# Attention scores of a hybrid decoder layer: three 64-row matmuls per block replaced by two 128-row matmuls with stacked query parts

## The chip, the cores and the metric

The kernel runs on one core of a Trainium2 chip. The metric is the device time of one execution in microseconds (us), as the median over several executions. Lower is better.

## The reference

The reference is one inference step of one decoder layer for a prompt of 512 positions and 8 sample positions of 2048 features: normalise, project to q, k, v and to the convolution's channels, dilated windowed attention over 16 heads of 64, a short gated convolution, an output projection, a gated feed-forward layer, and a per-layer embedding. What matters here is the score of the prompt's attention and the rows that are given back:

```
q = rms_norm(q.reshape(hs), q_norm)            # 16 heads of 64
k = rms_norm(k.reshape(hs), k_norm)
s = einsum('brnqhd,brnkhd->brnhqk', q, k) * HEAD_DIM ** -0.5 + bias
e = exp(s - max(s));  o = einsum('brnhqk,brnkhd->brnqhd', e, v) / sum(e)
outputs: y_prompt, y_sample, k_prompt (the keys), v_prompt (the values), ...
```

All is float32, and the kernel keeps that precision on TensorE by splitting each operand into a high part in fp32r (`hi`) and the rest (`lo`), and adding the products hi x hi, hi x lo and lo x hi.

## The kernel before

The work is laid out with features on the 128 partitions and the 520 positions along the free axis. Five engines run one program each and meet at semaphores: SP loads weights, ScalarE (ACT) writes the high part of each weight unit into `whi`, VectorE (DVE) writes the low part into `wlo`, TensorE (PE) multiplies, and GpSimd (POOL) keeps sums of squares and issues the stores and the smaller loads.

The first stage, "mixers", has eight head pairs j = 0 to 7. A pair has 12 weight units g = 0 to 11 (v, k, q and three convolution projections, two units each) of 48 matmuls of 260 columns. `whi` and `wlo` have four buffers, and ACT and DVE split unit g + 4 at step g. While pair j is projected, the attention of pair a = j - 1 is worked through, one slice after each unit (`attention(a, g)`); the last pair's attention lies in the convolution half of the output projection that follows. At g = 0 to 7 a score block is made: head e = g // 4 of the pair, query block qb = g % 4, against (qb + 1) x 128 keys, so 128, 256, 384 and 512 columns, twice. `products` issues hi x hi (L539), the weights `qhi` against `klo` (L540), and `qlo` against `khi` (L541). Their operands take 64 of the 128 partitions, those of the head. The same three lines, with 128 partitions, multiply values by probabilities (`vhi`, `vlo`, `pthi`, `ptlo`).

At g = 9, 10 and 11 of pair j (`heads`) the keys and queries of that pair are normalised, on DVE a reciprocal and a multiplication for each (L1405, L1407); ACT copies the high part of k (L936) and q (L918), DVE subtracts for the low part (L1374, L1330). PE transposes v and then k into one PSUM bank, ACT copies them to `v_nat` (L944) and `k_nat` (L956), which POOL stores to the outputs, and from `v_nat` come `vhi` (L949) and `vlo` (L1328). The next `attention(a, 0)` on PE begins, after unit 0 of the next pair, with

```
pe.wait_ge(s_root, 2 * a + 2)
pe.wait_ge(s_qk2, 2 * a + 2)     # klo and qlo of this pair written
```

The chain of one attention step is: PE scores, DVE scale and bias (L1260) and maximum (L1263), ACT exponential (L909), DVE reciprocal (L1267) and product (L1269), then after the next unit PE transposes the probabilities (L567).

Of the kernel before, what the change touches and what calls it, by code (L numbers as in the profile page):

```python
# [24 lines left out]
F32 = mybir.dt.float32  # L25
F32R = mybir.dt.float32r
# [4 lines left out]
P = 128  # L31
# [108 lines left out]
def build(nc, x_prompt, x_sample, p_prompt, p_sample, cache_k, cache_v, state_conv, rel_bias, g_mix,  # L140
# [57 lines left out]
    v_t = sb("v_t", [P, T], scope=mix)  # L198
    k_t = sb("k_t", [P, T], scope=mix)
    q_t = sb("q_t", [P, T], scope=mix)  # L200
    khi = sb("khi", [P, SEQ], F32R, mix)
    klo = sb("klo", [P, SEQ], F32R, mix)
    qhi = sb("qhi", [P, SEQ], F32R, mix)
    qlo = sb("qlo", [P, SEQ], F32R, mix)
    v_nat = sb("v_nat", [P, QB, P], scope=mix)
    k_nat = sb("k_nat", [P, QB, P], scope=mix)
    vhi = sb("vhi", [P, QB, P], F32R, mix)
    vlo = sb("vlo", [P, QB, P], F32R, mix)
    small_nat = sb("small_nat", [DEC + 2, 3, P], scope=mix)
# [58 lines left out]
    xb_lo = sb("xb_lo", [P, EARLY, 7, HALF], F32R, upper)  # L268
    up_t = sb("up_t", [P, 2, T], scope=upper)
    upper.close()  # L270


    after = ExitStack()
# [72 lines left out]

    s_sq, s_ssq, s_root, s_inv = sem("squared"), sem("heads_summed"), sem("root_ready"), sem("inverse_ready")
    s_qk, s_cols = sem("qk_normed"), sem("sample_cols")
    s_qkhi, s_qk2 = sem("qk_hi"), sem("qk_split")
    s_nat, s_natsb, s_vhi, s_v2 = sem("nat_transposed"), sem("nat_copied"), sem("v_hi"), sem("v_split")  # L350
    s_u, s_tap, s_conv = sem("u_ready"), sem("conv_tap"), sem("conv_ready")
    s_ident, s_sqs, s_zero, s_pad = (sem("identity_cleared"), sem("squares_step"), sem("squares_cleared"),
# [154 lines left out]
    def _(pe):  # L507
# [36 lines left out]
        def attention(a, g):  # L544
            if g in (3, 5, 7, 9):
                pair_of = (g - 3) // 2
                q0 = pair_of % 2 * 2
                if pair_of == 0:
                    pe.wait_ge(s_v2, a + 1)
                if pair_of == 2:  # L550
                    pe.wait_ge(s_o, 2 * a + 1)
                pe.wait_ge(s_pt2, 8 * a + (2 * pair_of + 2))
                for kb in (0, q0 + 1, *range(1, q0 + 1)):
                    skip = kb > q0
                    done = products(aux[:, BANK_O, (q0 + skip) * P:(q0 + 2) * P], vhi[:, kb, :], vlo[:, kb, :],
                                    pthi[:, kb, skip:2, :], ptlo[:, kb, skip:2, :], kb == 0,
                                    kb == max(q0, 1))
                done.then_inc(s_pv, 1)
            if 1 <= g <= 8:
                c = g - 1  # L560
                if c == 0:
                    pe.wait_ge(s_natsb, 5 * a + 5)
                else:
                    pe.wait_ge(s_pt2, 8 * a + c)
                pe.wait_ge(s_prob, 8 * a + (c + 1))
                for kb in range(c % QB + 1):
                    done = nc.tensor.transpose(aux[:, BANK_T, kb * P:(kb + 1) * P],  # L567
                                               prob[:, c % 2, kb * P:(kb + 1) * P], ident[:, :])
                done.then_inc(s_pt, 1)
            if g <= 7:  # L570
                e, qb = g // QB, g % QB
                if g == 0:
                    pe.wait_ge(s_root, 2 * a + 2)
                    pe.wait_ge(s_qk2, 2 * a + 2)
                else:
                    pe.wait_ge(s_biased, 8 * a + g)
                rows = slice(e * HD, (e + 1) * HD)
                done = products(aux[:, BANK_S, 0:(qb + 1) * P],
                                qhi[rows, qb * P:(qb + 1) * P], qlo[rows, qb * P:(qb + 1) * P],
                                khi[rows, 0:(qb + 1) * P], klo[rows, 0:(qb + 1) * P], True, True)  # L580
                done.then_inc(s_score, 1)
            if g in (1, 2):
                if g == 1:
                    pe.wait_ge(s_cols, 3 * a + 3)
                if g == 2:
                    pe.wait_ge(s_mul, 2 * a + 1)
                for b in range(4):
                    n = 4 * (g - 1) + b
                    done = nc.tensor.transpose(aux[:, BANK_D, b * P:(b + 1) * P],
                                               qkv_s[:, 0, n:n + 1].broadcast_to([P, P]), ident[:, :])  # L590
                done.then_inc(s_qb, 1)
            if g == 5:
                pe.wait_ge(s_key, 4 * a + 4)
                for t in range(KCACHE):
                    nc.tensor.transpose(aux[0:2 * DEC, BANK_D, t * P:(t + 1) * P], key_sc[:, t, :], ident[:, :])
                mm(aux[0:2 * DEC, BANK_D, PAST:PAST + 1], kq_pair[:, :, :], ones[:, 0:1],
                   start=True, stop=True).then_inc(s_str, 1)
            if g == 7:
                pe.wait_ge(s_row, 5 * a + 5)
                mm(aux[:, BANK_D, KCACHE * 2 * DEC:(KCACHE + 1) * 2 * DEC], ones[0:2 * DEC, :], new_diag[:, :],  # L600
                   start=True, stop=True)
                for t in range(KCACHE):
                    done = nc.tensor.transpose(aux[:, BANK_D, t * 2 * DEC:(t + 1) * 2 * DEC],
                                               row[:, t * P:(t + 1) * P], ident[0:2 * DEC, 0:2 * DEC])
                done.then_inc(s_str, 1)
            if g == 8:
                pe.wait_ge(s_pc, a + 1)
                pe.wait_ge(l_vc, 16 * a + 16)
                for b in range(DEC):
                    for t in range(KCACHE):  # L610
                        done = mm(aux[:, BANK_D, 2 * b:2 * b + 2], kv[:, KCACHE * b + t, :],
                                  p_cols[:, t, 2 * b:2 * b + 2], start=t == 0, stop=t == KCACHE - 1)
                done.then_inc(s_spv, 1)
# [269 lines left out]
    def _(act):  # L883
# [29 lines left out]
                on(row[:, :], row[:, :], ACT.Exp, bias=row_stats[:, 0:1], accum_out=row_stats[:, 1:2]  # L913
                   ).then_inc(s_sexp, 1)

        def q_hi(j):
            act.wait_ge(s_qk, 2 * j + 2)
            on(qhi[:, :], q_t[:, 0:SEQ], ACT.Copy).then_inc(s_qkhi, 1)  # L918

        def heads(j, a, g, last):  # L920
            if g == 7:
# [4 lines left out]
            if g == 9:  # L926
                act.wait_ge(s_ssq, 2 * j + 1)
                if a is not None:
                    act.wait_ge(s_qk, 2 * j)
                root_of(qk_rstd, HD).then_inc(s_root, 1)  # L930
                act.wait_ge(s_read, 6 * j + 3)
                on(sq[:, :], q_t[:, :], ACT.Square).then_inc(s_sq, 1)
                act.wait_ge(s_qk, 2 * j + 1)
                if a is not None:
                    act.wait_ge(s_score, 8 * a + 8)
                on(khi[:, :], k_t[:, 0:SEQ], ACT.Copy).then_inc(s_qkhi, 1)  # L936
            if g == 10:
                act.wait_ge(s_ssq, 2 * j + 2)
                root_of(qk_rstd, HD).then_inc(s_root, 1)
                act.wait_ge(s_nat, 2 * j + 1)  # L940
                if a is not None:
                    act.wait_ge(d_v, 16 * j)
                    act.wait_ge(d_small, 64 * j)
                on(v_nat[:, :, :], aux[:, BANK_T, :].rearrange("p (b f) -> p b f", b=QB), ACT.Copy).then_inc(s_natsb, 1)  # L944
                on(small_nat[0:DEC, 0, :], aux[0:DEC, BANK_O, 0:P], ACT.Copy).then_inc(s_natsb, 1)
                if a is not None:
                    act.wait_ge(s_pv, 4 * a + 4)
                act.wait_ge(s_natsb, 5 * j + 1)
                on(vhi[:, :, :], v_nat[:, :, :], ACT.Copy).then_inc(s_vhi, 1)  # L949
                if not last:  # L950
                    q_hi(j)
            if g == 11:
                act.wait_ge(s_nat, 2 * j + 2)
                if a is not None:
                    act.wait_ge(d_k, 16 * j)
                on(k_nat[:, :, :], aux[:, BANK_T, :].rearrange("p (b f) -> p b f", b=QB), ACT.Copy).then_inc(s_natsb, 1)  # L956
                on(small_nat[0:DEC, 1, :], aux[0:DEC, BANK_O, P:2 * P], ACT.Copy).then_inc(s_natsb, 1)
                on(small_nat[0:DEC + 2, 2, :], aux[0:DEC + 2, BANK_O, 2 * P:3 * P], ACT.Copy).then_inc(s_natsb, 1)
# [265 lines left out]
    def _(dve):  # L1224
# [97 lines left out]
        def norm_q(j):  # L1322

            norm_head(q_t, ROWS["q"], 2 * j + 1)
            V.tensor_copy(qkv_s[:, 0, :], q_t[:, SEQ:T]).then_inc(s_cols, 1)
            V.tensor_copy(qkv_s[:, 2, :], v_t[:, SEQ:T]).then_inc(s_cols, 1)
            dve.wait_ge(s_vhi, j + 1)
            V.tensor_tensor(vlo[:, :, :], v_nat[:, :, :], vhi[:, :, :].bitcast(F32), ALU.subtract).then_inc(s_v2, 1)  # L1328
            dve.wait_ge(s_qkhi, 2 * j + 2)
            V.tensor_tensor(qlo[:, :], q_t[:, 0:SEQ], qhi[:, :].bitcast(F32), ALU.subtract).then_inc(s_qk2, 1)  # L1330

        def heads(j, a, g, last):
            if a is None and g == 5:
# [31 lines left out]
            if g == 9:  # L1365
# [5 lines left out]
                norm_head(k_t, ROWS["k"], 2 * j)  # L1371
                V.tensor_copy(qkv_s[:, 1, :], k_t[:, SEQ:T]).then_inc(s_cols, 1)
                dve.wait_ge(s_qkhi, 2 * j + 1)
                V.tensor_tensor(klo[:, :], k_t[:, 0:SEQ], khi[:, :].bitcast(F32), ALU.subtract).then_inc(s_qk2, 1)  # L1374
            if g == 10:

                def tap(t):
# [7 lines left out]
                for n, t in enumerate((1, 0)):  # L1385
# [2 lines left out]
                                           ALU.mult, ALU.add).then_inc(s_tap, 1)  # L1388
                    V.scalar_tensor_tensor(conv[:, SEQ:T], old[:, :, t], tap(t), conv[:, SEQ:T],
                                           ALU.mult, ALU.add).then_inc(s_tap, 1)  # L1390
                if not last:
                    norm_q(j)
            if g == 11:
# [585 lines left out]
```

## Time and profile before

| what | value |
| --- | --- |
| median of 3 runs | 2640.67 us (2638.8 to 2643.58) |
| profiled execution, its own time | 2644.02 us |
| span of its instructions | 2642.5 us |
| PE busy | 2579.8 us, 98% |
| DVE busy | 1733.2 us, 66% |
| ACT busy | 908.0 us, 34% |
| mean granted TensorE clock | 0.982 |

Busy times are those of the profiled execution. An engine's share of the span says how full it is over all stages together; a single stage can be bound by another one. A granted clock of 1.00 is TensorE's full 2.4 GHz, 0.50 is 1.2 GHz.

### The profile page before, as it was taken

The page shows a single profiled execution, that of the slowest core. Times are in us where ns is not written, and L with a number is a line of the kernel's source. Part 1 is how long each engine was busy: PE and PEld are TensorE (multiplying, and loading weights), DVE is VectorE, ACT ScalarE, POOL GpSimd, SP SyncE. Part 2 cuts the span into 40 slices and gives each one's busy share as a digit, 9 for nine tenths or more (in the row PEclk, how much of TensorE's full clock was granted, in tenths as well). Part 3 has the DMA queues.
Part 4 walks back from the last instruction along what each step waited for, and adds up shares of the span by engine and source line. Part 5 has one row for each costly group of instructions (what it writes and reads, how often), then busy time and mean ns, then how long its engine had stood idle before and what let it go on. Part 6 is the DMA issues. An engine that isn't in the chain of part 4 may idle for free. (4 is left out here: it accounts for less than half of the span.)

```text
span 2642.5 us, 52849 instructions
## 1 busy us (share of the span) xinstructions
PE 2579.8 (98%) x20868; PEld 2539.4 (96%) x20868; DVE 1733.2 (66%) x2126; ACT 908.0 (34%) x1224; POOL 362.8 (14%) x387
## 2 busy tenths in 40 slices
PE   6999999999999998999999999999999999999998
PEld 6999999999999998999999999999999999999998
DVE  6556656665667698998988888888533322466332
ACT  3233323333333234444444444444332211232221
POOL 5201101111110260000000000000000000142001
PEclk8999999999999998999999999999999999999999
DMA  5734333333334343444544544444565543233331
GB/s 147 215 98 116 103 104 96 103 100 101 114 100 129 107 132 96 139 128 126 145 127 111 155 132 111 138 131 129 189 215 169 166 143 114 79 93 96 108 107 56
DMA packets 482064, 328.31 MB, mean 124 GB/s; under 512 B 19398, under 2 KB 458218, under 8 KB 480968
## 3 DMA queue, kind: packets, MB, share of 16 engines
q1 hardware_dynamic: 449296, 248.38, 33.4%
q0 software_dynamic: 28960, 75.33, 8.7%
q10 hardware_dynamic: 3744, 3.74, 0.5%
q8 instruction: 41, 0.67, 0.1%
q14 instruction: 23, 0.19, 0.0%
HBM read 286.80 MB, written 44.91 MB: 126 GB/s over the span
## 5 line engine op out<-in xcount | busy, mean ns | idle before, releaser
L1230 DVE TENSOR_TENSOR wlo<-wraw,whi 128x1024 fp32r<-128x1024 f32 (+1 forms) x276 | 334.5, 1212 | 511.5 <-ACT whi L891 511.2
L891 ACT ACTIVATE whi<-wraw 128x1024 fp32r<-128x1024 f32 (+1 forms) x276 | 285.2, 1033 | 805.0 <-PE acc L529 698.1
L745 PE MATMUL acc<-xb_hi,whi 128*128 128x260 f32 x1232 | 349.4, 284 | 10.6 <-DVE xb_lo L1557 10.6
L746 PE MATMUL acc<-xb_lo,whi 128*128 128x260 f32 x1232 | 349.6, 284 | 0.0
L745 PE MATMUL acc<-xa_hi,whi 128*128 128x260 f32 x1232 | 348.8, 283 | 0.6 <-DVE wlo L1509 0.6
L747 PE MATMUL acc<-xb_hi,wlo 128*128 128x260 f32 x1232 | 349.2, 283 | 0.0
L747 PE MATMUL acc<-xa_hi,wlo 128*128 128x260 f32 x1232 | 348.9, 283 | 0.0
L746 PE MATMUL acc<-xa_lo,whi 128*128 128x260 f32 x1232 | 348.8, 283 | 0.0
L525 PE MATMUL acc<-slots_a,whi 128*128 128x260 f32 x1536 | 321.8, 292 | 1.4 <-DVE slots_a L1238 1.2
L529 PE MATMUL acc<-slots_a,wlo 128*128 128x260 f32 x1536 | 315.7, 288 | 0.0
L527 PE MATMUL acc<-slots_a,whi 128*128 128x260 f32 x1536 | 314.0, 286 | 0.0
L525 PE MATMUL acc<-slots_b,whi 128*128 128x260 f32 x1408 | 287.9, 286 | 5.1 <-ACT hid L1153 2.6
L529 PE MATMUL acc<-slots_b,wlo 128*128 128x260 f32 x1408 | 285.2, 284 | 0.0
L527 PE MATMUL acc<-slots_b,whi 128*128 128x260 f32 x1408 | 283.4, 283 | 0.0
L1062 ACT ACTIVATE whi<-wraw 128x1024 fp32r<-128x1024 f32 x176 | 186.4, 1059 | 234.5 <-PE acc L747 125.2
L1509 DVE TENSOR_TENSOR wlo<-wraw,whi 128x1024 fp32r<-128x1024 f32 x176 | 215.3, 1223 | 69.9 <-ACT whi L1062 67.8
L525 PEld LDWEIGHTS acc<-slots_a,whi 128*128 128x128 f32 x1536 | 243.8, 194 | 6.1 <-issue 3.1
L745 PEld LDWEIGHTS acc<-xb_hi,whi 128*128 128x128 f32 x1232 | 233.4, 189 | 11.6 <-DVE xb_lo L1557 8.9
L527 PEld LDWEIGHTS acc<-slots_a,whi 128*128 128x128 f32 x1536 | 243.9, 194 | 0.0
L529 PEld LDWEIGHTS acc<-slots_a,wlo 128*128 128x128 f32 x1536 | 241.5, 193 | 0.0
L745 PEld LDWEIGHTS acc<-xa_hi,whi 128*128 128x128 f32 x1232 | 232.9, 189 | 0.9 <-DVE wlo L1509 0.8
L747 PEld LDWEIGHTS acc<-xb_hi,wlo 128*128 128x128 f32 x1232 | 232.9, 189 | 0.0
(298 smaller groups left out, 5181.5 us busy)
## 6 DMA issues: line engine op xcount, KB each, us to landing
wraw<-in_w_in SPq DMA_DIRECT2D x96, 512.0 KB, 4.0
blocks<-in_w_gate SPq DMA_DIRECT2D x88, 512.0 KB, 6.3
blocks<-in_w_up SPq DMA_DIRECT2D x88, 512.0 KB, 6.4
wraw<-in_w_down SPq DMA_DIRECT2D x48, 448.0 KB, 3.7
wraw<-in_w_out SPq DMA_DIRECT2D x32, 512.0 KB, 4.0
wraw<-in_w_ple_gate SPq DMA_DIRECT2D x32, 512.0 KB, 4.0
slots_b<-f_dram SPq DMA_DIRECT2D x28, 520.0 KB, 4.7
f_dram<-sig_t POOLq DMA_DIRECT2D x22, 520.0 KB, 3.3
```

Source lines behind the costliest of these rows:

```text
L525: mm(acc[:, slot, h, 0:HALF], w_h, x[:, 0, h * HALF:(h + 1) * HALF], start=begin, stop=False)
L527: mm(acc[:, slot, h, 0:HALF], w_h, x[:, 1, h * HALF:(h + 1) * HALF], start=False, stop=False)
L529: done = mm(acc[:, slot, h, 0:HALF], w_l, x[:, 0, h * HALF:(h + 1) * HALF], start=False, stop=end)
L745: mm(to, w_h, hi[:, n, X_OF[u], :], start=p == 0, stop=False)
L746: mm(to, w_h, lo[:, n, X_OF[u], :], start=False, stop=False)
L747: done = mm(to, w_l, hi[:, n, X_OF[u], :], start=False, stop=p == KP2 - 1)
L891: on(whi[:, u % HILO, 0:width], wraw[:, u % RAW, 0:width], ACT.Copy).then_inc(s_whi, 1)
L1062: on(whi[:, w % HILO, :], source, ACT.Copy).then_inc(s_whi, 1)
L1230: V.tensor_tensor(wlo[:, u % HILO, 0:width], wraw[:, u % RAW, 0:width], whi[:, u % HILO, 0:width].bitcast(F32), ALU.subtract).then_inc(s_w ...
L1509: V.tensor_tensor(wlo[:, w % HILO, :], source, whi[:, w % HILO, :].bitcast(F32), ALU.subtract).then_inc(s_wlo, 1)
```

## The change

The high and low parts of a head's queries are stacked on the 128 partitions of one tile: `q_both[e]` holds the high part of head e on the head's own 64 partitions and the low part on the other 64. The keys' high part of each head is laid on both halves (`k_hi2`), and the low part too (`k_lo2`). One matmul of 128 rows of `q_both[e]` against `k_hi2` then gives hi x hi + lo x hi, and one against `k_lo2` gives hi x lo + lo x lo. So a block has two matmuls of 128 rows in the place of three of 64, of the same column counts, and PE gets a wait on the second half of the high keys.

On ACT the one copy of the keys becomes four of 64 partitions (two before `s_qkhi`, two behind it) and the one of the queries two. On DVE the one subtraction for the keys becomes four and that for the queries two; `vlo` moves ahead of the queries' normalisation. To find the room, `k_nat` becomes the same tile as `v_nat`, so that ACT's copy of the natural keys at g = 11 waits for the store of the values to land and for `vlo`, and the copy of the natural values at g = 10 waits for the last pair's store of the keys. `q_both[0]` takes the place of a tile of `hid` that was stored to DRAM at the start, and its first writing waits for that store.

```diff
-    khi, klo, qhi, qlo: [P, SEQ]
-    k_nat = sb("k_nat", [P, QB, P], scope=mix)
+    k_hi2, k_lo2: [P, 2, SEQ]; q_both1: [P, SEQ]; q_both0 over a tile of hid
+    k_nat = v_nat
@@ TensorE, attention
+                    pe.wait_ge(s_khi2, a + 1)
-                done = products(aux[:, BANK_S, 0:(qb + 1) * P],
-                                qhi[rows, qb * P:(qb + 1) * P], qlo[rows, qb * P:(qb + 1) * P],
-                                khi[rows, 0:(qb + 1) * P], klo[rows, 0:(qb + 1) * P], True, True)
+                out, q = aux[:, BANK_S, 0:(qb + 1) * P], q_both[e][:, qb * P:(qb + 1) * P]
+                mm(out, q, k_hi2[:, e, 0:(qb + 1) * P], start=True, stop=False)
+                done = mm(out, q, k_lo2[:, e, 0:(qb + 1) * P], start=False, stop=True)
@@ ScalarE
-            on(qhi[:, :], q_t[:, 0:SEQ], ACT.Copy).then_inc(s_qkhi, 1)
+            if fresh:
+                act.wait_ge(d_spill, 64)
+            on(q_both[0][0:HD, :], q_t[0:HD, 0:SEQ], ACT.Copy)
+            on(q_both[1][HD:P, :], q_t[HD:P, 0:SEQ], ACT.Copy).then_inc(s_qkhi, 1)
-                on(khi[:, :], k_t[:, 0:SEQ], ACT.Copy).then_inc(s_qkhi, 1)
+                for e in range(2):
+                    rows = slice(e * HD, (e + 1) * HD)
+                    done = on(k_hi2[rows, e, :], k_t[rows, 0:SEQ], ACT.Copy)
+                done.then_inc(s_qkhi, 1)
+                for e in range(2):
+                    rows = slice((1 - e) * HD, (2 - e) * HD)
+                    done = on(k_hi2[rows, e, :], k_t[e * HD:(e + 1) * HD, 0:SEQ], ACT.Copy)
+                done.then_inc(s_khi2, 1)
@@ g == 10, before v_nat is written
+                    act.wait_ge(d_k, 16 * j)
@@ g == 11, before k_nat is written
+                act.wait_ge(d_v, 16 * j + 16)
+                act.wait_ge(s_v2, j + 1)
@@ VectorE
-            V.tensor_tensor(qlo[:, :], q_t[:, 0:SEQ], qhi[:, :].bitcast(F32), ALU.subtract).then_inc(s_qk2, 1)
+            dve.wait_ge(s_qkhi, 2 * j + 2)
+            for e in range(2):
+                rows, others = slice(e * HD, (e + 1) * HD), slice((1 - e) * HD, (2 - e) * HD)
+                done = V.tensor_tensor(q_both[e][others, :], q_t[rows, 0:SEQ], q_both[e][rows, :].bitcast(F32),
+                                       ALU.subtract)
+            done.then_inc(s_qk2, 1)
-                V.tensor_tensor(klo[:, :], k_t[:, 0:SEQ], khi[:, :].bitcast(F32), ALU.subtract).then_inc(s_qk2, 1)
+                for e in range(2):
+                    rows, others = slice(e * HD, (e + 1) * HD), slice((1 - e) * HD, (2 - e) * HD)
+                    for to in (rows, others):
+                        done = V.tensor_tensor(k_lo2[to, e, :], k_t[rows, 0:SEQ], k_hi2[rows, e, :].bitcast(F32),
+                                               ALU.subtract)
+                done.then_inc(s_qk2, 1)
@@ g == 10, after the convolution's taps and before norm_q(j); taken out of norm_q
+                v_lo(j)
```

## Rows read from the trace of the kernel before

**Rows 1.** Busy time and clock by stretch (us from the span's start)
```profile
139.60:142.80 3.20, 3.20 (x15) 2.98 (x16) 2.46 (x6) 0.80 (x3) 0.00 (x0) 0.50 0.54 152
318.00:410.00 92.00, 92.00 (x726) 88.34 (x725) 56.88 (x94) 29.19 (x52) 12.41 (x14) 0.98 0.35 103
```

**Rows 2.** Timeline of PE, start us and us, 512-column block of pair 2
```profile
338.69 0.40 PE L529 MATMUL acc<-slots_a,wlo 128*128 128x260 f32 x2
338.93 0.28 PE L539 MATMUL aux<-pthi,vhi 128*128 128x256 f32 x1
339.05 0.28 PE L540 MATMUL aux<-ptlo,vhi 128*128 128x256 f32 x1
...
339.56 0.52 PE L567 MATMUL aux<-ident,prob 128*128 128x128 f32 x3
340.01 0.50 PE L539 MATMUL aux<-khi,qhi 64*128 64x512 f32 x1
340.35 0.39 PE L540 MATMUL aux<-klo,qhi 64*128 64x512 f32 x1
340.58 0.39 PE L541 MATMUL aux<-khi,qlo 64*128 64x512 f32 x1
340.90 0.51 PE L525 MATMUL acc<-slots_c,whi 128*128 128x260 f32 x2
341.25 0.28 PE L527 MATMUL acc<-slots_c,whi 128*128 128x260 f32 x1
```

**Rows 3.** Timeline of PE, 128-column block
```profile
318.31 0.33 PE L539 MATMUL aux<-khi,qhi 64*128 64x128 f32 x1
318.47 0.27 PE L540 MATMUL aux<-klo,qhi 64*128 64x128 f32 x1
```

**Rows 4.** Timeline of DVE, end of pair 3's projections
```profile
391.10 0.69 DVE L1251 COPY hid<-aux 64x512 f32 x1
391.82 0.70 DVE L1235 TENSOR_TENSOR tmp<-acc,rstd 128x520 f32<-128x520 f32 x1
...
398.55 0.69 DVE L1374 TENSOR_TENSOR klo<-k_t,khi 128x512 fp32r<-128x512 f32 x1 [0.50 <-ACT khi L936]
399.50 1.23 DVE L1230 TENSOR_TENSOR wlo<-wraw,whi 128x1024 fp32r<-128x1024 f32 x1 [0.26 <-ACT whi L891]
...
407.51 0.68 DVE L1328 TENSOR_TENSOR vlo<-v_nat,vhi 128x512 fp32r<-128x512 f32 x1
408.11 0.68 DVE L1330 TENSOR_TENSOR qlo<-q_t,qhi 128x512 fp32r<-128x512 f32 x1
...
414.17 1.38 DVE L1269 TENSOR_SCALAR prob<-prob,stats 128x128 f32<-128x128 f32 x1
```

**Rows 5.** Timeline of ACT, the same stretch
```profile
397.89 0.64 ACT L936 ACTIVATE khi<-k_t 128x512 fp32r<-128x512 f32 x1 [5.64 <-DVE k_t L1407]
398.43 1.04 ACT L891 ACTIVATE whi<-wraw 128x1024 fp32r<-128x1024 f32 x1
...
407.36 0.63 ACT L918 ACTIVATE qhi<-q_t 128x512 fp32r<-128x512 f32 x1 [6.25 <-DVE q_t L1407]
...
408.84 0.58 ACT L956 ACTIVATE k_nat<-aux 128x512 f32<-128x512 f32 x1
```

**Rows 6.** Timeline of PE, pair 3's first score and next transposition
```profile
410.25 0.33 PE L539 MATMUL aux<-khi,qhi 64*128 64x128 f32 x1
...
416.60 0.27 PE L567 MATMUL aux<-ident,prob 128*128 128x128 f32 x1
```

**Rows 7.** Waits of PE: total us, times, longest us
```profile
PE acc L525 <- DVE slots_c L1238: 5.9, 3, 3.0
...
PE aux L567 <- DVE prob L1269: 2.8, 1, 2.8
...
PE aux L539 <- DVE qlo L1330: 1.5, 1, 1.5
```

**Rows 8.** Tile v_nat: landing of the values' stores
```profile
DMA to landing us min/median/max: 4.5/4.8/12.4
```

More of the change, by code:

```diff
@@ L200, in build @@
     q_t = sb("q_t", [P, T], scope=mix)
[L201 to L204, printed above, removed]
+    k_hi2 = sb("k_hi2", [P, 2, SEQ], F32R, mix)
+    k_lo2 = sb("k_lo2", [P, 2, SEQ], F32R, mix)
+    q_both1 = sb("q_both1", [P, SEQ], F32R, mix)
     v_nat = sb("v_nat", [P, QB, P], scope=mix)
-    k_nat = sb("k_nat", [P, QB, P], scope=mix)
+    k_nat = v_nat
     vhi = sb("vhi", [P, QB, P], F32R, mix)
@@ L270, in build @@
     upper.close()
+    early = ExitStack()
+    sb("below_q", [P, KT + KA - 1, T], scope=early)
+    q_both = (sb("q_both0", [P, SEQ], F32R, early), q_both1)
+    early.close()
     after = ExitStack()
@@ L348, in build @@
     s_qk, s_cols = sem("qk_normed"), sem("sample_cols")
-    s_qkhi, s_qk2 = sem("qk_hi"), sem("qk_split")
+    s_qkhi, s_khi2, s_qk2 = sem("qk_hi"), sem("k_hi_doubled"), sem("qk_split")
     s_nat, s_natsb, s_vhi, s_v2 = sem("nat_transposed"), sem("nat_copied"), sem("v_hi"), sem("v_split")
@@ L574, in attention @@
                     pe.wait_ge(s_qk2, 2 * a + 2)
+                    pe.wait_ge(s_khi2, a + 1)
                 else:
                     pe.wait_ge(s_biased, 8 * a + g)
-                rows = slice(e * HD, (e + 1) * HD)
-                done = products(aux[:, BANK_S, 0:(qb + 1) * P],
-                                qhi[rows, qb * P:(qb + 1) * P], qlo[rows, qb * P:(qb + 1) * P],
-                                khi[rows, 0:(qb + 1) * P], klo[rows, 0:(qb + 1) * P], True, True)
+                out, q = aux[:, BANK_S, 0:(qb + 1) * P], q_both[e][:, qb * P:(qb + 1) * P]
+                mm(out, q, k_hi2[:, e, 0:(qb + 1) * P], start=True, stop=False)
+                done = mm(out, q, k_lo2[:, e, 0:(qb + 1) * P], start=False, stop=True)
                 done.then_inc(s_score, 1)
@@ L914, in attention, with q_hi @@
                    ).then_inc(s_sexp, 1)
-        def q_hi(j):
+        def q_hi(j, fresh=False):
             act.wait_ge(s_qk, 2 * j + 2)
-            on(qhi[:, :], q_t[:, 0:SEQ], ACT.Copy).then_inc(s_qkhi, 1)
+            if fresh:
+                act.wait_ge(d_spill, 64)
+            on(q_both[0][0:HD, :], q_t[0:HD, 0:SEQ], ACT.Copy)
+            on(q_both[1][HD:P, :], q_t[HD:P, 0:SEQ], ACT.Copy).then_inc(s_qkhi, 1)
         def heads(j, a, g, last):
@@ L950, in heads @@
                 if not last:
-                    q_hi(j)
+                    q_hi(j, a is None)
             if g == 11:
@@ L1326, in norm_q, with v_lo @@
             V.tensor_copy(qkv_s[:, 2, :], v_t[:, SEQ:T]).then_inc(s_cols, 1)
+            dve.wait_ge(s_qkhi, 2 * j + 2)
[4 more added lines that the diff above has]
+            done.then_inc(s_qk2, 1)
+        def v_lo(j):
             dve.wait_ge(s_vhi, j + 1)
             V.tensor_tensor(vlo[:, :, :], v_nat[:, :, :], vhi[:, :, :].bitcast(F32), ALU.subtract).then_inc(s_v2, 1)
-            dve.wait_ge(s_qkhi, 2 * j + 2)
-            V.tensor_tensor(qlo[:, :], q_t[:, 0:SEQ], qhi[:, :].bitcast(F32), ALU.subtract).then_inc(s_qk2, 1)
         def heads(j, a, g, last):
```

## The prediction

> **What bounds the kernel now.** I read the table by stretch first. In the 92.0 us from 318 to 410, which are one turn of the mixers' loop, PE is busy for all 92.0 us, DVE for 56.9 and ACT for 29.2 [rows 1]. So PE sets the pace, and what counts is how far apart its matmuls start. The waits of PE come next: in the mixers they are single events at the first pair (1.5 us for `qlo`, 2.8 us for the first probabilities) and at the transition to the output projection, where one of the three waits of L1238 stands, 2.6 of its 5.9 us [rows 7]. None repeats with the loop. Then the timeline of PE gives the price of a block, and those of DVE and ACT at g = 9 to 11 give what the new work may take before PE notices.
>
> **PE's gain.** Prices are distances between starts, as PE overlaps its matmuls. Between 128-row matmuls: 0.24 us for two of 260 columns (338.69 to 338.93), 0.12 for one of 256 (338.93 to 339.05) [rows 2]. That also holds across the step from the projection into the values' products, from one bank and operand to another. The 64-row block has more. Three transpositions lie 0.12 apart (0.52 busy less the 0.27 of one, halved), which makes 0.36, but the first score starts 0.45 after the first of them: 0.09 lost on entering. The first score matmul takes 0.34 to the next start, where the second with the same 512 columns takes 0.23: 0.11 lost. The third takes 0.32: 0.09 lost on leaving. The first two matmuls of the next unit take 0.35 in place of 0.24: 0.11, of which I count 0.10 [rows 2]. In the 128-column block the first takes 0.16 where the 128-column transpositions take 0.12, so only some 0.05 is lost there [rows 3]. All four losses stand at or just behind a change between 128 and 64 rows, and none at the values' products, which have 128.
>
> The change takes out one matmul per block: 0.11 to 0.12, 0.12, 0.17 and 0.23 us for the four widths (0.17 is my estimate between 256 and 512 columns), 0.63 a head, 1.27 a pair, 10.2 us over eight pairs. It takes out the change of rows too: 0.09 + 0.05 + 0.09 + 0.10 = 0.33 at 128 columns, some 0.33 at 256 (where short transpositions follow), 0.38 at 384 and 0.39 at 512, less 0.19 for the one block of a pair behind which 16-row matmuls come anyway. That is 2 x 1.43 - 0.19 = 2.67 a pair, 21.4 us over eight. The whole gain on PE is 3.94 us a pair and 31.6 us in all. Bounds: 10.2 if the losses stay, 33 if the last one goes too.
>
> A page speaks against the second part. The Trainium skill, "TensorE: Matmul & The Clock Gate", section "Step-by-step: what each phase is for", says that a weight load is timed by columns and that the row count does not matter; by that alone only the 10.2 us would be saved. "TensorEngine Tiling (Array Packing)", section "Key Properties", says that a change of the tiling mode drains the engine, which would give the 31.6. The trace sides with the second [rows 2], but it does not show a 128-row score block.
>
> **DVE's and ACT's new work.** Reference is pair 3. ACT's 512-column copy starts 0.54 before the next instruction (397.89 to 398.43) [rows 5]; I take the same for 64 partitions. DVE waits for the second copy: the first subtraction starts at 399.09 in place of 398.55. DVE's subtractions of 512 columns are 0.60 apart (407.51 to 408.11), but the one 64-partition instruction is followed 0.72 later (391.10 to 391.82) [rows 4]. With 0.72 four of them end the stretch at 401.97, where the next split `wlo` started at 399.50: 2.47 late. `whi` is not later than that: two more copies and its own 1.04 bring it to about 401.1 [rows 5]. `vlo` before `norm_q` adds 0.60, so `q_t` is 3.07 late. Then DVE waits for two copies of ACT, which begin at 407.36 + 3.07 = 410.43 and end at 411.60, and two subtractions end at 413.03. The PE score started at 410.25 [rows 6]; `qlo` had ended at 408.79, so there was 1.46 of cover. It is used up, and PE waits 2.8 us. With a spacing of 0.60 in place of 0.72 it would be 2.2; I take 2.8, because the row with 64 partitions is nearest. Before, these subtractions cost nothing since PE was still in unit 0; with the cover gone every further 0.1 us is on PE's path.
>
> The Trainium skill, "VectorE: DVE Perf Modes", section "Two Vector instructions with no wait between them", gives a model by which an instruction that starts in another group of partitions begins only when the earlier one is done. That fits the 0.72; with it PE waits 2.8, without it 2.2.
>
> What is late next: DVE's split, two products and the softmax of block 0. The probabilities were ready at 414.17 + 1.38 = 415.55 [rows 4], PE asked at 416.60 [rows 6]. DVE is 4.2 late, PE with its wait and its shorter block 2.5, so about 0.1 to 0.6 more is waited for, less if that product runs shorter than 1.38 at another moment. I take 0.2. From the next unit on DVE follows PE again. That is 3.0 us a pair for pairs 1 to 6, 18 us (bounds 13 and 21).
>
> **First and last pair.** At the first pair `qlo` is on PE's path already (1.5 us waited), so the full 3.6 us appear there; but the following 2.8 us wait for the first probabilities takes most of it back, as it hangs on a weight load. The values' store took up to 12.4 us to land [rows 8], that is the first pair's, and ACT would stand on it before the natural keys until about 135, which delays the exponential by 1 to 3. I take 2 us together (0 to 4). In pair 7 there is no attention behind the chain but the convolution operands' low parts, on which PE already waits 2.6 [rows 7]: 3.07 late at once, and the two half subtractions that follow later make it about 4. I take 4 us (3 to 4.5).
>
> **The shared natural tile.** In the loop `v_nat` is written shortly after ACT's split of 398.43 [rows 5], by 400.5, and its store lands some 5 us later [rows 8], before 409 even with 2 us more on ACT and POOL's issue; the keys' copy was at 408.84 [rows 5] and comes at about 412. `vlo` is then long done. No stall from pair 1 on. If it stood, POOL's store of the keys would wait behind it and nothing of PE for a unit. The wait on `d_spill` is over long before, and the copy of the natural values waits for a store issued 80 us ago.
>
> **Clock.** The 2.8 us wait of the first pair was followed by a stretch at 0.50, 1.2 GHz, from 139.6 to 142.8 [rows 1], the 1.5 us wait by none [rows 7]. 3.2 us at half cost 1.6 us. The new waits of 2.8 us lie near the upper one. I take it that three of the six are followed by such a stretch, 4.8 us (0 to 10).
>
> **Sum.** -31.6 + 18 + 2 + 4 + 4.8 = -2.8, and with the other half-clock stretches of the loop no longer falling where they did, some -4. The profiled execution took 2644.0 us (span 2642.5, 1.5 around it), so 2640 there. The median of the runs is 3.3 lower, 2640.7, so I forecast 2636.5, rounded to 2636.
>
> **Rivals.**
> *The waits cost less or leave the clock alone.* Spacing of 0.60 and no stretch at half clock: -31.6 + 14 + 1 + 3.3 = -13, 2628; with 2.8 us waits and no clock effect -8, 2633. For it: the spacing of full-width subtractions; against it: the row with 64 partitions and the half clock behind 2.8 us.
> *The clock falls in every pair.* -31.6 + 20 + 3 + 4 + 10 = +5, 2646. For it: the one wait of this size whose clock I show was followed by one; against: PE did not wait this long at a fixed place of every pair before, so one event is all there is.
> *The losses around score blocks have nothing to do with the row count.* Slower: only 10.2 is saved, the 24 us of waits stay, some less: +12, 2653. From waits of 24 us on the edit loses as soon as less than 24 of the 31.6 come. Against it: the values' products show none of the four losses.
> *The chain of `qk2` is hidden anyway.* Then -28, 2613. The 1.46 us of cover speaks against it.
>
> **Chances.** Forecast (within some 4 us of 2636) 0.45; waits cheaper or clock untouched 0.25; clock in every pair 0.15; losses stay 0.10; all hidden 0.05. The range leaves out the last two and a little more: 2623 to 2646. The likeliest case alone spans 2632 to 2641. A measurement tells 0.2%, 5.3 us, from no change: faster is 0.25 + 0.05 and a third of the forecast's, 0.45; same the rest of the forecast's and half of the clock's, 0.38; slower the other half of that and the losses that stay, 0.17.
>
> **What would show it.** Score blocks with 128-row matmuls starting 0.12 and 0.23 apart, and no 0.35 behind them: the gain. A wait of PE on the queries' subtraction of 2 to 3 us, seven times, in the list of waits: the cost. The period of a pair, 92.0 now, near 91 with no fall and 92.7 with one. The forecast is wrong if that wait is missing, if the natural keys' copy waits for a store in each pair, or if the 64-partition instructions take much longer than 0.7 us.

## The result, and the profile after

The changed kernel takes 2660.86 us (median of 4 runs, 2657.59 to 2662.93) beside 2640.78 us for the kernel before: ratio 1.0072, 95% interval 1.006 to 1.0085. It is 0.7% slower, where 2636 was forecast in a range that ended at 2646. The profiled execution has a span of 2656.0 us and a mean granted clock of 0.975, against 2642.5 and 0.982. The two profiled executions lie 13.5 us apart and the medians 20.1: the one before was the slowest of its four, the one after the fastest of its four. What the traces explain below is the 13.5.

The score block first. The timeline of TensorE after shows the 512-column block that answers to [rows 2]:

```profile
340.30 0.52 PE L572 MATMUL aux<-ident,prob 128*128 128x128 f32 x3
340.57 0.48 PE L584 MATMUL aux<-k_hi,q_both 128*128 128x512 f32 x1
340.89 0.40 PE L585 MATMUL aux<-k_lo,q_both 128*128 128x512 f32 x1
341.13 0.40 PE L530 MATMUL acc<-slots_c,whi 128*128 128x260 f32 x2
341.37 0.40 PE L532 MATMUL acc<-slots_c,whi 128*128 128x260 f32 x2
```

From the first transposition to the second step of the next unit it is 1.07 us, where [rows 2] have 339.56 to 341.25, 1.69. That is 0.62 saved: 0.62 had been worked out, 0.23 for the removed matmul and 0.39 for the change of rows. The two matmuls of the next unit are 0.24 apart again.

Then the waits of TensorE (line, releaser: total us, times, longest), to be read beside [rows 7]. "issue" stands where the trace names no releaser; the timelines below name it.

```profile
PE aux L584 <- issue: 21.3, 7, 3.7
...
PE acc L530 <- DVE slots_c L1256: 8.9, 4, 3.0
...
PE aux L644 <- ACT small_nat L961: 3.0, 1, 3.0
...
PE acc L530 <- DVE tmp L1253: 2.5, 1, 2.5
...
PE aux L572 <- DVE prob L1287: 1.0, 1, 1.0
```

L584 is the first score matmul of a pair. It waited once before, 1.5 us; now seven times. The timelines of DVE, ACT and PE after, at the end of pair 2's projections, show the chain ahead of it (start us, us):

```profile
303.57 2.79 DVE L1401 TENSOR_TENSOR k_lo<-k_t,k_hi 64x512 fp32r<-64x512 f32 x4 [1.14 <-ACT k_hi L946]
306.39 1.23 DVE L1248 TENSOR_TENSOR wlo<-wraw,whi 128x1024 fp32r<-128x1024 f32 x1
...
310.01 0.69 DVE L1354 TENSOR_TENSOR vlo<-v_nat,vhi 128x512 fp32r<-128x512 f32 x1
310.62 3.40 DVE L1435 RECIPROCAL tmp<-tmp 128x520 f32<-128x520 f32 x1
...
316.14 1.38 DVE L1348 TENSOR_TENSOR q_both<-q_t,q_both 64x512 fp32r<-64x512 f32 x2 [1.06 <-ACT q_both L926]
```

```profile
302.26 1.27 ACT L946 ACTIVATE k_hi<-k_t 64x512 fp32r<-64x512 f32 x2 [5.63 <-DVE k_t L1437]
303.56 1.27 ACT L950 ACTIVATE k_hi<-k_t 64x512 fp32r<-64x512 f32 x2
...
314.84 0.63 ACT L925 ACTIVATE q_both<-q_t 64x512 fp32r<-64x512 f32 x1 [7.28 <-DVE q_t L1437]
315.48 0.63 ACT L926 ACTIVATE q_both<-q_t 64x512 fp32r<-64x512 f32 x1
316.13 1.06 ACT L896 ACTIVATE whi<-wraw 128x1024 fp32r<-128x1024 f32 x1
317.10 0.58 ACT L974 ACTIVATE v_nat<-aux 128x512 f32<-128x512 f32 x1
```

```profile
317.63 0.44 PE L584 MATMUL aux<-k_hi,q_both 128*128 128x128 f32 x1 [2.89 <-issue]
```

The reader sees four subtractions take 2.8 us, `vlo` before the reciprocal, two copies of 0.64 each, and two subtractions that end at 317.52; 0.1 us later the score begins. L974 is the natural keys' copy into the shared tile: it follows the split `whi` without a gap, so the waits for the values' store and for `vlo` cost nothing here.

The clock is the last and largest part. Busy time by stretch after (stretch, its us, busy of PE, PEld, DVE, ACT, POOL, then the granted clock, the DMA share, GB/s):

```profile
413.10:508.70 95.60, 92.63 (x716) 91.32 (x716) 59.36 (x98) 31.89 (x58) 12.42 (x14) 0.93 0.35 99
60.00:905.00 845.00, 809.28 (x6339) 796.06 (x6338) 525.50 (x838) 279.65 (x481) 118.02 (x141) 0.95 0.40 113
412.40:419.00 6.60, 5.86 (x27) 5.89 (x28) 5.69 (x9) 3.82 (x8) 4.94 (x7) 0.50 0.55 142
474.00:480.40 6.40, 6.40 (x30) 6.40 (x31) 0.77 (x5) 0.00 (x0) 1.93 (x2) 0.50 0.48 125
```

A turn of the loop takes 95.6 us, where 92.0 were taken before, at a clock of 0.93 in place of 0.98 [rows 1]. The last two rows are the two places of the turn that ran at 1.2 GHz: at and behind the wait for the first score (it ended at 413.1), and at the sample's matmuls of two columns at g = 8. Before, the second place had one such stretch, half as long, in each turn, and the first had none; below, the two kinds are called the long and the short stretch. Summed over the clock's records between 60 and 905 us (the mixers and the convolution half of the output projection), TensorE was at half clock for 37.5 us before and for 88.8 us after. The 51.2 us more lie at three places: 34.1 at and behind the first scores (a long stretch in five of the six turns that follow the first pair), 13.7 at the two-column matmuls, 3.4 at the first pair. If PE were busy in all of it, they would be 25.6 us; it is busy in 82.9 of the 88.8 us (the stretch at the first score begins while PE still waits) and in all of the 37.5, which makes 22.7.

One of the six waits was followed by full clock, that of the pair at 226.1:

```profile
226.10:232.50 6.40, 6.31 (x52) 6.11 (x52) 5.36 (x8) 3.23 (x8) 5.26 (x7) 1.00 0.63 162
```

From there to the next first score, with the short stretch alone, as in the turns before, it took 91.53 us.

### The profile page after: what moved, and what is told of

It reads as the page before. It is cut to its first block and busy times, and to the rows that moved or that the text cites. A ratio compares the mean times of both kernels' runs of the same rounds, so it can differ in the third digit from the quotient of the medians.

```text
span 2656.0 us, 52808 instructions
## 1 busy us (share of the span) xinstructions
PE 2566.3 (97%) x20804; PEld 2543.7 (96%) x20804; DVE 1752.5 (66%) x2158; ACT 929.2 (35%) x1256; POOL 363.0 (14%) x387
## 5 line engine op out<-in xcount | busy, mean ns | idle before, releaser
L530 PE MATMUL acc<-slots_a,whi 128*128 128x260 f32 x1536 | 326.4, 295 | 2.4 <-DVE slots_a L1256 2.2
L532 PE MATMUL acc<-slots_a,whi 128*128 128x260 f32 x1536 | 318.1, 289 | 0.0
L530 PEld LDWEIGHTS acc<-slots_a,whi 128*128 128x128 f32 x1536 | 250.7, 199 | 4.9 <-DVE slots_a L1256 3.4
L532 PEld LDWEIGHTS acc<-slots_a,whi 128*128 128x128 f32 x1536 | 248.5, 197 | 0.0
```

Of the source, the lines that this page charges most:

```text
L530: mm(acc[:, slot, h, 0:HALF], w_h, x[:, 0, h * HALF:(h + 1) * HALF], start=begin, stop=False)
L532: mm(acc[:, slot, h, 0:HALF], w_h, x[:, 1, h * HALF:(h + 1) * HALF], start=False, stop=False)
```

## The experiments

Every kernel was timed against the kernel before on the same chip. "Half clock" is the sum just described, "first scores" the wait in total at the first score of the pairs, from each kernel's profiled execution. "Without clock" is that execution's span less half of the half-clock time, as a difference to the kernel before (2642.5 - 18.75 = 2623.75).

| kernel | median us | ratio (interval) | half clock us | first scores us | without clock |
| --- | --- | --- | --- | --- | --- |
| before | 2641 | 1 | 37.5 | 1.5 | 0 |
| changed kernel | 2660.86 | 1.0072 (1.006 to 1.0085) | 88.8 | 21.3 | -12.1 |
| e1 two 128-row matmuls alone | 2610.41 | 0.9892 (0.9873 to 0.9911) | 27.3 | 1.5 | -29.6 |
| e2 three 128-row matmuls | 2625.52 | 0.9949 (0.9933 to 0.9966) | 44.4 | 1.5 | -23.1 |
| e3 two 64-row matmuls | 2638.75 | 0.9993 (0.9982 to 1.0004) | 47.8 | 1.5 | -13.0 |
| e4 preparation alone | 2673.55 | 1.0124 (1.0098 to 1.015) | 51.2 | 20.8 | +21.0 |
| e5 shared natural tile alone | 2641.84 | 0.9997 (0.9987 to 1.0006) | 37.5 | 1.5 | +1.6 |
| f1 changed, wait filled | 2637.87 | 0.9986 (0.9977 to 0.9996) | 44.4 | filled | -6.7 |
| h1 changed, 1 us more work a pair | 2648.24 | 1.0027 (1.0011 to 1.0042) | 44.4 | 19.7 | -3.5 |
| h2 changed, 0.5 us more | 2644.70 | 1.0015 (1.0005 to 1.0024) | 54.6 | 19.8 | -9.9 |
| h3 before, 1 us more | 2649.67 | 1.0028 (1.0015 to 1.004) | 51.2 | 1.5 | +3.3 |
| g1 changed, shorter chain | 2623.53 | 0.9927 (0.9911 to 0.9944) | 44.4 | 3.1 | -24.2 |
| g2 g1 with two pieces moved | 2613.84 | 0.9899 (0.9882 to 0.9916) | 34.1 | 1.3 | -29.2 |

The last column is a rough aid, good to some 7 us: it counts the clock from 60 to 905 us alone and takes TensorE as busy in all of it. With TensorE's busy time at half clock counted instead, and the stretches behind 905 us taken in (18.3 us before, 10.5 after), the changed kernel stands at -5.3 in place of -12.1. The lengths of single turns that hold the same stretches are the sharper measure.

**e1, e2, e3: the three parts of TensorE's gain.** Each edits only the score block of the kernel before:

```diff
 e1
+                out, q = aux[:, BANK_S, 0:(qb + 1) * P], qhi[:, qb * P:(qb + 1) * P]
+                mm(out, q, khi[:, 0:(qb + 1) * P], start=True, stop=False)
+                done = mm(out, q, klo[:, 0:(qb + 1) * P], start=False, stop=True)
 e2: the three products as before, with all 128 rows of qhi, qlo, khi and klo
 e3: as e1, with the 64 rows of the head in qhi, khi and klo
```

> The kernel before, with only the score block changed on TensorE: two matmuls of 128 rows (qhi against khi, qhi against klo), operands prepared as before; the scores of the two heads run into one another and the product with qlo is left out. Theory A (the edit's gain on TensorE is real, and the time after was lost in the 3 us waits for the queries' subtraction and in half-clock stretches that these waits set off): 31.6 us faster than before, 2609, no wait at the first score from the second pair on, half-clock time in the mixers as before (38 us). Theory B (the new score blocks themselves bring the clock down, or save less than their starts show): half-clock time well above 38 us, time above 2625.

> The kernel before with its three score matmuls on all 128 rows; the scores of the two heads run into one another. Only the change between 128 and 64 rows is gone. If the distances lost around a score block belong to the row count: 21 us faster, 2619. If they belong to something else: 2641.

> The kernel before with the third score matmul (qlo against khi) left out and 64 rows kept. Only the columns are saved: 10 us faster, 2631. If the rows do not matter and the removed matmul carries the loss around a block with it: 2619 or less.

e1 came at 2610.41, 30.5 us below before. The waits and one turn of its loop:

```profile
PE aux L567 <- DVE prob L1268: 4.0, 2, 3.0
...
PE aux L578 <- DVE qlo L1329: 1.5, 1, 1.5
```

```profile
485.40:573.50 88.10, 88.10 (x717) 86.95 (x716) 56.77 (x95) 29.20 (x52) 12.39 (x15) 0.98 0.37 107
```

The turn takes 88.1 us at the same 0.98, 3.9 us less than before; 3.94 a pair had been worked out. e2 is 15.4 us faster than before as measured (21 expected), e3 2.2, which cannot be told from nothing (10 expected). Both have more half clock than before, by 6.9 and 10.3 us, and that hides part of the saving. Turns that hold one short stretch, as those before do, leave the clock out; e2's and e3's are

```profile
314.90:404.30 89.40, 89.40 (x725) 88.16 (x724) 56.77 (x95) 29.21 (x52) 12.43 (x15) 0.98 0.37 106
```

```profile
222.10:312.80 90.70, 90.70 (x716) 87.12 (x715) 56.78 (x95) 29.22 (x52) 12.42 (x15) 0.98 0.36 104
```

From first score to first score such a turn is 91.95 us before, 88.07 in e1, 89.38 in e2 and 90.71 in e3. So the rows alone save 2.57 a turn (2.67 worked out), the removed matmul alone 1.24 (1.27), both together 3.88. The rows carry two thirds of the gain. The Trainium skill, "TensorEngine Tiling (Array Packing)", section "Key Properties", says that a change of the tiling mode drains the engine; e2's 2.57 us a turn agree with it, though no run shows the drain as such.

**e4: the preparation alone.** The cut leaves out the waits that the extra tiles need.

```diff
 ScalarE and VectorE of the kernel before, pair j
+                for e in range(2): on(khi[rows, :], k_t[rows, 0:SEQ], ACT.Copy)       # in the place of one copy
+                for e in range(2): on(k_nat[rows, :, :], k_t[rows, 0:SEQ] ..., ACT.Copy)
+                for e in range(2):
+                    for to in (klo[rows, :], gate_t[rows, 0:SEQ]):
+                        done = V.tensor_tensor(to, k_t[rows, 0:SEQ], khi[rows, :].bitcast(F32), ALU.subtract)
+                v_lo(j)                                                              # before norm_q(j)
+            for e in range(2): ... qhi[rows, :] ... qlo[rows, :]                      # copies and subtractions of q
```

> The kernel before with the old score matmuls, but with the changed kernel's amount of preparation: ScalarE copies the keys in four halves and the queries in two, VectorE subtracts the keys in four halves and the queries in two, vlo ahead of the queries' normalisation (the extra halves go to tiles that are free). Theory A: waits of about 3 us at the first score of seven pairs and some 1 us behind it, and half-clock time in the mixers of about 80 to 90 us in place of 38: 24 us of waits and 20 to 25 of clock, 2685. Theory B (the clock falls because of the new matmuls): the waits alone, 2663, half-clock time near 38 us. Theory C (where the narrow 2-column matmuls lie against the clock's grid decides): half-clock time between the two, and not at the waits.

It measured 2673.55, 32.6 us above before. Its waits and two of its turns behind the first score:

```profile
PE aux L539 <- DVE qlo L1341: 20.8, 7, 3.6
```

```profile
420.90:430.20 9.30, 9.27 (x74) 8.96 (x75) 7.01 (x11) 4.29 (x9) 5.25 (x7) 1.00 0.55 142
515.80:525.10 9.30, 9.30 (x52) 9.03 (x52) 5.29 (x8) 3.03 (x6) 5.23 (x7) 0.66 0.53 142
```

The waits are those of the changed kernel, now with their releaser. But the clock did not do what theory A said: 51 us at half clock, not 80 to 90, and the time lies between A's 2685 and B's 2663, as theory C has it. The same wait of 2.9 us is followed by full clock in three of the six turns behind the first pair and by a long stretch in the other three, of which the two rows show one each. So the new matmuls are not needed for a fall, and the wait alone does not decide.

**e5: the shared natural tile alone.** `k_nat = v_nat` with its waits, `vlo` ahead only in the last pair.

> The kernel before with only the shared tile of natural values and keys, and its waits on the stores. If the sharing costs nothing, as forecast for all pairs but the first: 2641, no wait on TensorE beyond those of before. If its waits are on the path: 2645 or more, with a longer wait for the first probabilities in the first pair.

2641.84 beside 2641.29 for the kernel before, ratio 0.9997: nothing that can be measured. The first pair's wait for the first probabilities is 3.7 us in its trace and was 2.8.

**f1: the wait filled.**

```diff
                     pe.wait_ge(s_root, 2 * a + 2)
+                    if not isinstance(a, int):
+                        for n in range(24):
+                            mm(aux[:, BANK_S, 0:HALF], slots_c[:, n % 8, 0, 0:P], slots_c[:, n % 8, 0, 0:HALF],
+                               start=True, stop=True)
                     pe.wait_ge(s_qk2, 2 * a + 2)
```

> The changed kernel, in which TensorE runs 24 matmuls of 260 columns into a free bank (2.9 us, results unused) in the place where it waits for the queries' subtraction; the wait itself, 3.1 us a pair, stays lost. Theory A (idle time there brings the clock down): no half-clock stretch begins at the first score; the interval from the first to the second score is about 6.4 us in place of 8.8 in every pair, and the narrow matmuls set off one stretch or none in place of two; about 2640, 20 us below the changed kernel. Theory B (the clock falls for another reason): 2660 as the changed kernel.

23 us below the changed kernel, 2637.87. The timeline of TensorE in f1, and the stretch behind:

```profile
409.95 3.07 PE L581 MATMUL aux<-slots_c 128*128 128x260 f32 x24
413.00 0.33 PE L588 MATMUL aux<-k_hi,q_both 128*128 128x128 f32 x1
```

```profile
413.00:419.40 6.40, 6.33 (x52) 6.13 (x52) 5.38 (x8) 3.24 (x8) 5.22 (x7) 1.00 0.63 163
```

The score starts 3.05 us late as before, so the wait's own price is still paid. The stretch that took 8.8 us at 0.66 in five of the changed kernel's turns takes 6.4 at 1.00 in all six of f1. No pair of the loop starts its scores at half clock.

**h1, h2, h3: more work in a turn.** Eight matmuls of 260 columns (four in h2) behind the first score of a pair, in the changed kernel (h1, h2) and in the kernel before (h3):

```diff
                 done.then_inc(s_score, 1)
+                if g == 0 and not isinstance(a, int):
+                    for n in range(8):
+                        mm(aux[:, BANK_D, 0:HALF], slots_c[:, n, 0, 0:P], slots_c[:, n, 0, 0:HALF],
+                           start=True, stop=True)
```

> The changed kernel with 8 more matmuls of 260 columns (1 us, results unused) behind the first score of seven pairs; waits unchanged. If half-clock time is set by the waits alone: 7 us slower, 2668. If the pair's period of 95.5 us had come to lie fixed against the clock's steps, with two stretches at both places: the place shifts from pair to pair, half-clock time falls below the 89 us of the changed kernel, and the time is below 2668, down to 2650.

> The changed kernel with 4 more matmuls of 260 columns (0.5 us, results unused) behind the first score of seven pairs. If any shift frees the pair's period from the place where four half-clock lengths fall in it: between 2642 and 2655. If the period comes back to 95.5 us because the clock takes up the slack: 2660 as the changed kernel.

> The control for the same filler in the kernel before: 8 more matmuls of 260 columns (1 us) behind the first score of seven pairs. If the filler only costs its own time: 2648. If the clock's stretches move as they did in the changed kernel: anywhere from 2641 to 2660, with half-clock time other than 38 us.

With 1 us more work in seven pairs the changed kernel is 12.6 us faster, with 0.5 us more 16.2 us; the intervals of the ratios lie apart from its own. That is what had been expected if the position decides; if the waits alone did, h1 would have taken 2668. The kernel before, with the same filler, is 8.4 us slower, close to the filler's own 7; but its half-clock time is 51.2 and not 38, so the shift moved its stretches too. h1's waits, its wait at 410.4 and what follows, and one turn:

```profile
PE aux L584 <- issue: 19.7, 7, 2.9
```

```profile
413.70:505.90 92.20, 89.28 (x724) 87.94 (x724) 59.29 (x98) 31.83 (x58) 12.44 (x14) 0.98 0.36 103
413.70:420.70 7.00, 7.00 (x59) 7.00 (x60) 5.33 (x8) 3.06 (x7) 5.24 (x7) 1.00 0.68 178
410.40:413.60 3.20, 0.34 (x3) 0.13 (x2) 2.07 (x5) 2.67 (x4) 0.00 (x0) 1.00 0.00 0
```

The wait is as long as in the changed kernel, and the clock stays at 1.00 through it and after it. The turn takes 92.2 us with more work in it than the 95.5 us turn. From first score to first score, the changed kernel's turns 3 to 6 are all 95.52 to 95.54 us long, each with half clock at both places; those of h1 are 92.2 from the second on and have it at one. So the changed kernel's turns had a length at which both places fell badly each time, and a shift of half a microsecond was enough to leave it.

**What in the position decides.** The traces of all runs answer this together. In each trace the clock's records begin at multiples of one common step. In the turns of the changed kernel, e4, h1 and h2 behind the first pair, TensorE stands idle for 2.86 to 2.95 us at the first score 24 times. The 11 waits that end 0.5 to 1.0 us behind a step are all followed by half clock, which begins at that step; the 13 that end 1.2 to 1.7 us behind one are not. The changed kernel's five lie at 0.77 to 0.94, h1's six at 1.3 to 1.55. In f1 two filled waits, those that end at 321.47 and 594.49 us, lie at 0.75 and 0.70, and neither is followed by half clock. The two-column matmuls follow the same kind of order: of the 104 groups of 32 in the 13 traces, the 25 that start 0.24 to 1.26 us behind a step are followed by a long stretch, the 14 that start at 1.36 to 1.78 by none, and the other 65 by a short one. The changed kernel's turns with a long stretch have theirs at 1.16 to 1.26, those of the kernel before at 1.8 to 3.1. This was read from the traces afterwards; no run moved one place alone by a chosen amount.

**g1 and g2: the same products with a shorter chain.** g1 keeps the stacked operands:

```diff
-                    for to in (rows, others): ... k_lo2[to, e, :] ...      # VectorE: own half only, a signal per half
+            act.wait_ge(s_qk2, 2 * j + 1)                                # ScalarE, ahead of the queries' copies
+            for part in (k_hi2, k_lo2):
+                for e in range(2):
+                    done = on(part[others, e, :], part[rows, e, :].bitcast(F32), ACT.Copy)
+            done.then_inc(s_khi2, 1)
-                v_lo(j)                                                  # back between norm_head and q's subtractions
```

g2 adds, on VectorE, `norm_q(j)` before the last tap of the convolution, and the gated product `conv * gate` of a pair behind `attention(a, 0)` of the next turn.

> The changed kernel with a shorter chain to the first score, the same results: VectorE subtracts only each head's own half of the keys, ScalarE copies both second halves in the 6 us in which it stood idle before the queries, each half has its own signal, and vlo comes back behind the queries' normalisation, where VectorE would wait for ScalarE. Chain some 1.4 us later than before where the cover is 1.46. Theory A: wait at the first score 0 to 0.6 us, half-clock time in the mixers below 50 us, 2612 (the bound from the TensorE part alone is 2610). Theory B (the stacked operands cost something else too): 2630 or more.

> The kernel of the shorter chain, with two pieces of VectorE's work moved out of the way of the first score and the first probabilities: the last convolution tap behind the queries' normalisation (0.9 us) and the convolution's gated product behind the first attention step of the next pair (0.7 us); same results. The 0.35 us wait at the first score and the 0.7 us wait at the first probabilities of each pair should go: 7 us faster than the shorter chain, and with one half-clock stretch per pair in all, 2611, the bound of the TensorE part alone. Rival: the two waits go but the clock's stretches lie otherwise, 2620.

g1 measured 2623.53; its remaining waits, and one turn of g2:

```profile
PE aux L572 <- DVE prob L1288: 4.4, 8, 1.0
...
PE aux L584 <- issue: 3.1, 6, 2.3
```

```profile
399.20:487.20 88.00, 88.00 (x716) 86.84 (x716) 57.40 (x96) 33.14 (x59) 12.38 (x14) 0.98 0.38 108
```

g1's first score starts 0.3 us late in a pair of the loop and the first probabilities 0.7 us (the first score had 0 to 0.6 expected, the second was not foreseen); with 44 us at half clock it lies 11.5 above the 2612 expected. g2 has neither wait in the loop, a turn of 88.0 as in e1, and measures 2613.84, ratio 0.9899 (0.9882 to 0.9916): 1.0% faster than before and 47 us faster than the changed kernel.

## Why the prediction was wrong

**The gain on TensorE: right.** 31.6 us were worked out; e1 has 30.5 as measured. By turns that hold the same stretches, the parts of 2.67 and 1.27 us a pair stand against 2.57 (e2) and 1.24 (e3), and the 3.94 against 3.88 (e1). Inside the 512-column block the prediction was right in the sum only, which was luck: the 0.11 us that it counted as lost in the first score matmul stays with 128 rows (0.32 to the next start, against 0.23 worked out), and 0.09 more than worked out comes back between the transpositions and the score (0.27 against 0.36).

**The chain to the first score: right, a little short.** A wait of 2.8 us was forecast and 3.1 is lost. ScalarE's 64-partition copies begin 0.64 apart, not the 0.54 taken from [rows 5]; VectorE's four subtractions take 0.70 each, as the 0.72 of [rows 4] said. The wait behind it, for the first probabilities, had been taken as 0.2; in f1 the interval from the first score to the second is 6.4 against 6.0 in e1, so 0.4. Together 3.5 a pair and 21 over six, where 18 stood. The turn of the changed kernel with the short stretch alone bears the sum out: 91.95 - 3.88 + 3.1 + 0.4 = 91.57, and 91.53 was measured.

**First and last pair: right.** First pair: 3.0 + 3.7 + 1.0 of waits against 0.9 + 1.5 + 2.8, 2.5 us for a term of 2. Transition: L1256 and L1253 wait 8.9 + 2.5 against 5.9 + 0.9, 4.6 for a term of 4. Adding up gains and waits without clock gives -31.6 + 21 + 2.5 + 4.6 = -3.5; the trace gives -5.3 with the clock taken out by TensorE's busy time and to the end of the execution. Five of the six 0.4 in the 21 are not paid in the changed kernel: in a turn that starts at half clock TensorE asks later and does not wait for the first probabilities. That makes -5.5.

**The shared tile: right.** No cost that can be measured (e5), and no wait in the loop.

**The clock: the step that failed.** The text said "I take it that three of the six are followed by such a stretch, 4.8 us (0 to 10)". The term was too small by a factor of nearly five: 22.7 us by TensorE's busy time, 25.6 by the clock's records alone. It fell short in three ways. The stretch behind a wait was twice as long as the one in [rows 1], and it came in five of the six turns, not three: 34.1 us at half clock, of which TensorE was busy for 29.9, so 15 us at the very place that was priced. The two-column matmuls at g = 8, which had a short stretch in every turn before, had a long one in five: 6.8 us more. The prediction had put that place at a gain of 1 us ("no longer falling where they did"). The first pair makes up the last 1 us. Per turn the changed kernel loses 4.0 us against a turn of f1 with one short stretch (95.5 against 91.5), and 2.4 of them lie behind the first score (8.8 against 6.4). And the turns are alike, so that what happens in one happens in all: from the third turn on they took 95.5 us with both places at half clock. The rival "the clock falls in every pair" had the mechanism and +5, with 10 us for the clock; it too priced one place only, with the short stretch.

h1, h2 and e4 show that a wait of 2.9 us is not enough for a fall: it depends on where the wait and the two-column matmuls come in time. f1 shows that without idle time no fall begins at the score, also at positions where every unfilled wait brought one. That the positions of the changed kernel are bad ones in both places, and those of h1 good ones, is chance; nothing in the edit aims at it.

## What to carry to other kernels

Stacking two 64-row operands on 128 partitions saved more by sparing TensorE the change of row count between neighbouring matmuls (some 0.32 us a block) than by the matmul it removed; look at the distance between starts on both sides of such a block. Work that makes an operand must be set against the cover ahead of its first reader (here 1.46 us of cover, and queries that are ready some 4.5 us later), and an engine that stands idle in the same stretch is the place for the copies. Where a loop's turns are identical, price the granted clock over the whole turn, not at the new wait alone; compare turns that hold the same half-clock stretches; and try a small shift of work before judging an edit by one timing.

## What the runs showed of the hardware that had not been expected

More work made the kernel faster: 0.5 us more in each of seven pairs took 16.2 us off, while the half-clock time fell from 88.8 to 54.6 us. A 2.9 us idle stretch of TensorE left the clock at 1.00 in every turn of h1 and in three turns of e4, and was followed by half clock in three others, 0.66 over the next 9.3 us. Which it was went in all 24 cases with where the wait ended against the clock's common step, and so it did for all 104 groups of two-column matmuls. With all matmuls at 128 rows, the start of a 512-column score lay 0.27 us behind the first of three transpositions and its successor 0.32 behind it, where 0.45 and 0.34 had been with 64 rows.
